# Two-layer hybrid decoder trunk: epsilon on VectorE, weight splits ahead of the last silu, last down products by column halves, GpSimd's residual products moved

## The chip, the cores and the metric

The kernel runs on one core of a Trainium2 chip, with its engines TensorE (PE), VectorE (DVE), ScalarE (ACT), GpSimd (POOL) and SyncE (SP, which only issues DMAs here). The metric is the device time of one execution in microseconds, the median of several runs.

## The reference

x is (1, 256, 1024) float32. Layer 0 mixes with a causal pooling, layer 1 with sliding-window attention. Each layer has three steps, so there are four feed-forward blocks (FFN 0 to 3, width 2816), two mixers and six layer norms (norm 0 to 5):

```python
def layer_norm(x, g, b):
    mu = jnp.mean(x, -1, keepdims=True); xc = x - mu
    var = jnp.mean(xc * xc, -1, keepdims=True)
    return xc * lax.rsqrt(var + LN_EPS) * g + b
def post_norm(x, sub, g, b):
    return layer_norm(DEEPNORM_ALPHA * x + sub, g, b)
for i in range(2):
    x = post_norm(x, 0.5 * swiglu(x, gate[i,0], up[i,0], down[i,0]), g[i,0], b[i,0])
    mix = pool_mixer(...) if i == 0 else swa_sink_attention(...)
    x = post_norm(x, mix, g[i,1], b[i,1])
    x = post_norm(x, 0.5 * swiglu(x, gate[i,1], up[i,1], down[i,1]), g[i,2], b[i,2])
```

## The kernel before, in words

The 256 tokens are two tiles, t = 0 and 1. To keep float32 accuracy nearly every product is made of three (`three`, L1057 to L1059): each operand is split into a high part (ACT copies it to fp32r: `g_hi` L459, `d_hi` L467, `xT_hi` L510, `hT_hi` L475) and a low part (DVE subtracts: `g_lo` L720, `d_lo` L724, `xT_lo` L806, `hT_lo` L733).

An FFN has 22 units of 128 columns. For each unit PE makes gate and up (48 products, `gate_up`), ACT takes the silu (L471), DVE multiplies it by the up half (`hf` L728), both split the result, and PE adds `ffn_down` into four PSUM banks: token tile t by column half h, 512 columns each, 3 products for each half. Units 0 and 1 use the raw weights with unsplit x (L1073) and need no split; units 2 to 21 do. On ACT and on DVE, `unit(f, u)` does, in program order: silu or `hf` of u, `g_split` of unit u+2, the split of h, `d_split` of unit u+1. After the last unit, `g_split(f+1, 2)` stands on ACT ahead of the transposed copies of the norm; on DVE its two halves stand as fillers in the norm (in norm 0 the two `d_split`s of the pooling weights do), between the variance and the wait for GpSimd.

SP issues every weight load in one fixed order (L263 on). Gate and up come as pairs of units (a chunk, 2 MB), down as pairs (1 MB). Each load waits for the split that frees its buffer. Between FFN 0 and FFN 1 the order is: pooling weights; gate/up of units 0 and 1 of FFN 1; down of units 0 and 1 (L252), which waits until `d_lo` of all 22 units of FFN 0 is done; then gate/up of units 2 and 3 (L245), which waits for `g_lo` of unit 21; then down of units 2 and 3.

A norm runs, for each t: DVE adds residual and product by column halves (L758) with `bn_stats` behind each (L759), then `bn_aggr` (L765); GpSimd adds epsilon (L356) and takes the power -1/2 (L358); DVE normalises both halves (L774), which count up `xn_done`; PE transposes (L1123) or, in the pool stage, multiplies by the band matrices (L890 for t=0, L894 for t=1); DVE and ACT copy the transposed tile with gain and bias (L800, L499). The pool stage then needs `xT_lo` from L843 on DVE. Norms 0 and 3 prepare the residual of the mixer on GpSimd: a product (`residual_mult`, L315) and a sum (`residual_add`, L319) for each t, of 1024 columns; `ax_done` counts them. At an FFN's end PE's order is: down of unit 21 for t=0, then of units 19, 20, 21 for t=1, each with both column halves.

Of the kernel before, what the change touches and what calls it, by code (L numbers as in the profile page):

```python
# [66 lines left out]
def trunk_kernel(nc, x, positions, ln_g, ln_b, w_gate, w_up, w_down, pool_w, pool_b, pool_scale,  # L67
# [8 lines left out]
    with ExitStack() as ctx:  # L76
# [70 lines left out]
        var_done = sem("var_done")  # L147
# [71 lines left out]
        prevT = xf[:, 1, 2:3, :]  # L219

# [80 lines left out]
        def _(gp):  # L301
# [19 lines left out]
            for n in range(6):  # L321
# [25 lines left out]
                if n == 3:  # L347

                    X, G, src = split_unit(None, 1)
                    gp.wait_ge(g_hi_done, 2 * X + 1)  # L350
                    gp.wait_ge(g_lo_done, 2 * X)
                    gp.tensor_tensor(g_half(g_lo, X, 0), src(G, 0), g_half(g_hi, X, 0).bitcast(f32), ALU.subtract).then_inc(g_lo_done, 1)
# [98 lines left out]
        def _(act):  # L451
# [25 lines left out]
            def unit(f, u, it=0):  # L477

                silu_of(f, u, it)
                if 1 <= u < UNITS - 2:  # L480
                    g_split(f, u + 2, it)
                elif f == 2 and u == UNITS - 2:
                    g_split(None, 0)
# [6 lines left out]
            def channel_major(e):  # L490

                for t in range(TT):
# [29 lines left out]
            for f in range(FFNS):  # L522
# [13 lines left out]
                if f == 0:  # L536
# [53 lines left out]
        def attention_dve(dve, link, note, g_split, d_split):  # L590
# [88 lines left out]
            g_split(None, 4)  # L679
            chunk(1, 0)  # L680
# [20 lines left out]
        def _(dve):  # L701
# [11 lines left out]
            def g_split(f, u, it=0, halves=(0, 1)):  # L713

                X, G, src = split_unit(f, u)
                for half in halves:
                    dve.wait_ge(g_hi_done, 2 * X + half + 1 + 8 * it)
                    if halves == (1,):
                        dve.wait_ge(g_lo_done, 2 * X + 1)
# [15 lines left out]
            def unit(f, u, it=0):  # L735

                h_of(f, u, it)
                if 1 <= u < UNITS - 2:
                    g_split(f, u + 2, it)
                elif f == 2 and u == UNITS - 2:  # L740
                    g_split(None, 0)
# [12 lines left out]
            def statistics(n, t, coef, early=None):  # L754

                for h in range(2):
                    dve.wait_ge(acc_done, 4 * n + 2 * t + h + 1)
                    link(dve.scalar_tensor_tensor(xn[:, t, HALVES[h]], ACC[t][h], coef, ax[:, t, HALVES[h]], ALU.mult, ALU.add))  # L758
                    last = dve.bn_stats(stats[:, h, :], xn[:, t, HALVES[h]])  # L759
                    if h == 0:  # L760
                        note(last)
                        if early:
                            early()
                link(last)
                dve.bn_aggr(mv[:, t, :], stats[:, :, :].rearrange("p a b -> p (a b)")).then_inc(stat_done, 1)  # L765

            def normalise(n, t, coef, filler=None, early=None):

                statistics(n, t, coef, early)
                if filler:  # L770
                    filler(t)
# [4 lines left out]

            def normalise_out(n, t, coef):

                statistics(n, t, coef)
# [41 lines left out]
            for f in range(FFNS):  # L821
# [14 lines left out]
                if f == 0:  # L836

                    for t in range(TT):
                        normalise(0, t, 0.5, filler=lambda t: d_split(D_POOL + t))
# [6 lines left out]
                    for t in range(TT):  # L846
                        dve.wait_ge(ax_done, 2 + t + 1)
                        normalise(1, t, 1.0, filler=lambda t: g_split(1, RAW_UNITS, halves=(t,)))
                        channel_major(1, t)
                    for t in range(TT):  # L850
                        x_lo(1, t)
                elif f == 1:
                    for t in range(TT):
                        normalise(2, t, 0.5, filler=lambda t: g_split(2, RAW_UNITS, halves=(t,)))
                        channel_major(2, t)
                    for t in range(TT):
                        x_lo(2, t)
                elif f == 2:

                    normalise(3, 0, 0.5, filler=lambda t: g_split(None, 1, halves=(1,)))  # L860
                    channel_major(QKV_EVENT, 0)
                    normalise(3, 1, 0.5, early=lambda: x_lo(QKV_EVENT, 0))
                    channel_major(QKV_EVENT, 1)
                    x_lo(QKV_EVENT, 1)
                    attention_dve(dve, link, note, g_split, d_split)
                    for t in range(TT):
                        dve.wait_ge(ax_done, 8 + t + 1)
                        normalise(4, t, 1.0, filler=lambda t: g_split(3, RAW_UNITS, halves=(t,)))
                        channel_major(4, t)
                    for t in range(TT):  # L870
                        x_lo(4, t)
# [40 lines left out]
        def attention_pe(pe, three, down, transposes, rest_of_ffn):  # L912
# [98 lines left out]
            rest_of_ffn()  # L1011
# [197 lines left out]
```

## Time and profile before

| | |
|---|---|
| median of 3 runs | 919.36 us (918.04 to 919.42) |
| span of the profiled execution (first to last instruction) | 916.1 us |
| median less that span (what lies around it; no time of its own is given for the profiled execution) | 3.26 us |
| PE busy | 875.6 us (96%) |
| DVE / ACT / POOL busy | 540.4 / 380.1 / 76.3 us |
| mean granted TensorE clock | 0.992 |

Busy times of PE are of pipelined instructions, so they overlap; the starts of neighbouring records tell the pace. In the timelines a row merges neighbouring instructions of one kind, and the bracket tells the idle time before it and who ended it.

### The profile page before, as it was taken

The numbers are of one execution on the slowest core, as the hardware profiler recorded it, in microseconds if no ns is written. First come the engines' busy times: TensorE is split into PE (matmuls) and PEld (weight loads), VectorE is DVE, ScalarE is ACT, GpSimd is POOL, SyncE is SP. The second block draws the span as 40 slices with busy tenths as digits, with TensorE's granted clock in tenths as the row PEclk, the third lists the DMA queues.
The fourth block names the chain that finished last, engine by engine and source line by source line (L and its number), as shares of the span: only waits on it lengthen the run. The fifth ranks groups of instructions, "written<-read, shape, count | busy, mean of one in ns | idle before, by whom it ended". The sixth has DMA issues, their size and how long they took to land.

```text
span 916.1 us, 14933 instructions
## 1 busy us (share of the span) xinstructions
PE 875.6 (96%) x5954; PEld 805.0 (88%) x5954; DVE 540.4 (59%) x758; ACT 380.1 (41%) x622; POOL 76.3 (8%) x71
## 2 busy tenths in 40 slices
PE   6999999997999999999999999988999999999995
PEld 6999999986999999998999999976766899999994
DVE  1764455488674455447665545568687775445445
ACT  2444344322444344333434433435575434434430
POOL 0020000066100000001040000023000100000001
PEclk9999999999999999999999999999999999999998
DMA  9886546254485555660865565450127096555501
GB/s 293 304 289 219 183 160 207 97 176 141 170 301 184 197 172 181 211 202 2 275 239 184 173 217 175 161 218 15 42 101 254 20 311 234 183 189 177 184 1 46
DMA packets 116275, 162.30 MB, mean 177 GB/s; under 512 B 3968, under 2 KB 97760, under 8 KB 116240
## 3 DMA queue, kind: packets, MB, share of 16 engines
q1 hardware_dynamic: 112656, 152.06, 49.2%
q0 software_dynamic: 2496, 9.44, 2.8%
q8 instruction: 24, 0.39, 0.2%
q10 hardware_dynamic: 1088, 0.32, 0.1%
q14 instruction: 11, 0.09, 0.0%
HBM read 160.75 MB, written 1.05 MB: 177 GB/s over the span
## 4 chain that ended last, share of the span: by engine, by line
PE 82%; DVE 10%; ACT 3%; POOL 2%; issue 1%; DMA 1%; SPq 0%; POOLq 0%; DVEq 0%; ACTq 0%
PE ps L1057 25%; PE ps L1058 25%; PE ps L1059 25%; PE ps L1073 5%; DVE stats L759 2%; DVE xn L758 2%; DMA raw_g<-in_ffn_w_up 1%; POOL rstd L356 1%; DVE xn L774 1%; PE ps L1123 1%; PE ps L943 1%; ACT silu L403 1%; PE ps L934 1%; PE ps L937 1%; POOL rstd L358 1%
## 5 line engine op out<-in xcount | busy, mean ns | idle before, releaser
L1059 PE MATMUL ps<-xT_hi,g_lo 128*128 128x256 f32 x1280 | 362.2, 283 | 0.0
L1058 PE MATMUL ps<-xT_lo,g_hi 128*128 128x256 f32 x1280 | 362.2, 283 | 0.0
L1057 PE MATMUL ps<-xT_hi,g_hi 128*128 128x256 f32 x1280 | 361.8, 283 | 0.0
L1057 PEld LDWEIGHTS ps<-xT_hi,g_hi 128*128 128x128 f32 x1280 | 245.4, 192 | 3.2
L1058 PEld LDWEIGHTS ps<-xT_lo,g_hi 128*128 128x128 f32 x1280 | 245.4, 192 | 3.1
L1059 PEld LDWEIGHTS ps<-xT_hi,g_lo 128*128 128x128 f32 x1280 | 245.4, 192 | 0.0
L720 DVE TENSOR_TENSOR g_lo<-raw_g,g_hi 128x1024 fp32r<-128x1024 f32 x171 | 206.5, 1247 | 42.0 <-ACT g_hi L459 41.9
L471 ACT ACTIVATE silu<-ps 128x256 f32<-128x256 f32 x88 | 33.8, 384 | 393.0 <-PE ps L1059 386.1
L728 DVE TENSOR_TENSOR hf<-silu,ps 128x256 f32<-128x256 f32 x88 | 37.0, 421 | 263.0 <-ACT silu L471 263.0
L459 ACT ACTIVATE g_hi<-raw_g 128x1024 fp32r<-128x1024 f32 x172 | 172.0, 1052 | 4.9 <-PE ps L943 4.4
L1057 PE MATMUL ps<-d_hi,hT_hi 128*128 128x512 f32 x352 | 138.7, 394 | 2.0 <-DVE hT_lo L733 2.0
L1058 PE MATMUL ps<-d_lo,hT_hi 128*128 128x512 f32 x352 | 137.9, 392 | 0.0
L1059 PE MATMUL ps<-d_hi,hT_lo 128*128 128x512 f32 x352 | 137.0, 389 | 0.0
L724 DVE TENSOR_TENSOR d_lo<-raw_d,d_hi 128x1024 fp32r<-128x1024 f32 x98 | 122.8, 1254 | 2.6 <-ACT d_hi L467 2.6
L467 ACT ACTIVATE d_hi<-raw_d 128x1024 fp32r<-128x1024 f32 x98 | 102.7, 1049 | 3.1 <-PE ps L1059 3.0
L1059 PEld LDWEIGHTS ps<-d_hi,hT_lo 128*128 128x128 f32 x352 | 66.1, 188 | 14.5
L1057 PEld LDWEIGHTS ps<-d_hi,hT_hi 128*128 128x128 f32 x352 | 66.4, 189 | 14.0 <-DVE hT_lo L733 2.4
L1058 PEld LDWEIGHTS ps<-d_lo,hT_hi 128*128 128x128 f32 x352 | 66.4, 189 | 10.6
L1073 PE MATMUL ps<-xf,raw_g 128*128 128x128 f32 x512 | 61.7, 282 | 3.8 <-DMA raw_g<-in_ffn_w_up 3.2
L1073 PEld LDWEIGHTS ps<-xf,raw_g 128*128 128x128 f32 x512 | 60.1, 197 | 5.4 <-DMA raw_g<-in_ffn_w_up 3.4
L733 DVE TENSOR_TENSOR hT_lo<-hf,hT_hi 128x256 fp32r<-128x256 f32 x88 | 43.5, 494 | 5.3 <-ACT hT_hi L475 5.3
L475 ACT ACTIVATE hT_hi<-hf 128x256 fp32r<-128x256 f32 x88 | 35.9, 408 | 11.9 <-DVE hf L728 11.9
(137 smaller groups left out, 548.9 us busy)
## 6 DMA issues: line engine op xcount, KB each, us to landing
raw_d<-in_ffn_w_down SPq DMA_DIRECT2D x87, 512.0 KB, 4.0
raw_g<-in_ffn_w_gate SPq DMA_DIRECT2D x43, 1024.0 KB, 5.3
raw_g<-in_ffn_w_up SPq DMA_DIRECT2D x43, 1024.0 KB, 7.8
raw_g<-in_attn_w_qkv SPq DMA_DIRECT2D x6, 1024.0 KB, 6.6
raw_d<-in_attn_w_o SPq DMA_DIRECT2D x8, 512.0 KB, 3.7
gb<-in_ln_g POOLq DMA_DIRECT2D x6, 512.0 KB, 5.2
gb<-in_ln_b POOLq DMA_DIRECT2D x6, 512.0 KB, 6.3
xn<-in_x SPq DMA_DIRECT2D x2, 512.0 KB, 7.2
```

What stands on the lines that cost most here:

```text
L459: act.activation(g_half(g_hi, X, half), src(G, half), ACT.Copy).then_inc(g_hi_done, 1)
L467: act.activation(d_hi[:, E % D_SLOTS, :], raw_d[:, (E // 2) % 2, E % 2, :], ACT.Copy).then_inc(d_hi_done, 1)
L471: act.activation(silu[:, u % 2, :], ps[:, WORK + u % 2, 0:S], ACT.Silu).then_inc(silu_done, 1)
L475: act.activation(hT_hi[:, (D0[f] + u) % D_SLOTS, :], hf[:, u % 2, :], ACT.Copy).then_inc(h_hi_done, 1)
L720: dve.tensor_tensor(g_half(g_lo, X, half), src(G, half), g_half(g_hi, X, half).bitcast(f32), ALU.subtract).then_inc(g_lo_done, 1)
L724: dve.tensor_tensor(d_lo[:, E % D_SLOTS, :], raw_d[:, (E // 2) % 2, E % 2, :], d_hi[:, E % D_SLOTS, :].bitcast(f32), ALU.subtract).then_in ...
L728: dve.tensor_tensor(hf[:, u % 2, :], silu[:, u % 2, :], ps[:, WORK + u % 2, S:2 * S], ALU.mult).then_inc(hf_done, 1)
L733: dve.tensor_tensor(hT_lo[:, slot, :], hf[:, u % 2, :], hT_hi[:, slot, :].bitcast(f32), ALU.subtract).then_inc(h_lo_done, 1)
L1057: pe.matmul(out_, l_hi, r_hi, start=start, stop=False)
L1058: pe.matmul(out_, l_hi, r_lo, start=False, stop=False)
L1059: return pe.matmul(out_, l_lo, r_hi, start=False, stop=stop)
L1073: last = pe.matmul(ps[:, WORK + u % 2, m * S + t * P:m * S + (t + 1) * P], raw_unit(G, m)[:, k, :], xf[:, t, k, :], start=i == 0, stop=i = ...
```

## The change

1. *Norm.* DVE adds epsilon (one instruction on 128x1 after `bn_aggr`), GpSimd only takes the power. `layer_norm` on DVE: the first residual sum of t=1 stands ahead of the wait for GpSimd of t=0; the fillers are gone from between the variance and that wait. The `d_split`s of the pooling weights follow norm 0, `g_split(3, 2)` follows norm 4 on DVE.
2. *Splits ahead of the last silu.* For FFN 0 and 1, ACT and DVE do `g_split(f+1, 2)` ahead of the silu and of `hf` of unit 21.
3. *Down products.* For t=1 the last three units go column half by column half. FFN 2's last product for t=1 is no longer held back behind the transposes; the first qkv products are reordered.
4. *GpSimd.* In norm 0 the sum of t=0, and product and sum of t=1, wait until t=1 is normalised. In norm 3, t=0's two are made ahead of t=1's power; t=1's two move to DVE in the attention part; the `g_lo` half that GpSimd made goes to DVE.
5. ACT splits x (`x_hi`) of t=0 straight behind its copies in norms 1, 2 and 4 too.

```diff
+        def next_split(f, u, it):
+            if 1 <= u < UNITS - 2:
+                return f, u + 2, it
+            if f == 2 and u == UNITS - 2:
+                return None, 0
+            if f < 2 and u == UNITS - 1:
+                return f + 1, RAW_UNITS
+            return None
...
@@ GpSimd
-                    gp.tensor_scalar(rstd[:, t, 0:1], mv[:, t, 1:2], EPS, None, ALU.add).then_inc(var_done, 1)
-                    gp.wait_ge(var_done, 2 * n + t + 1)
                     gp.tensor_tensor(rstd[:, t, 1:2], rstd[:, t, 0:1], mhalf[:, :], ALU.pow).then_inc(rstd_done, 1)
                     if step is not None and t == 0:
                         residual_mult(n, 0)
-                if step is not None:
+                        if n == 3:
+                            residual_add(step, 0)
+                if n == 0:
+                    gp.wait_ge(xn_done, 4)
                     residual_add(step, 0)
                     residual_mult(n, 1)
                     residual_add(step, 1)
@@ ScalarE, unit (VectorE's is changed likewise around h_of)
+                ahead = next_split(f, u, it)
+                if ahead and u == UNITS - 1:
+                    g_split(*ahead)
                 silu_of(f, u, it)
...
@@ VectorE
+            def layer_norm(n, coef, e=None, ready=None, behind_first=None, early_lo=False):
+                if ready:
+                    ready(0)
+                half_statistics(0, 0, residual_sum(n, 0, 0, coef))
+                variance(0, half_statistics(0, 1, residual_sum(n, 0, 1, coef)))
+                if ready:
+                    ready(1)
+                first = residual_sum(n, 1, 0, coef)
+                normalise(n, 0)
+                if e is not None:
+                    channel_major(e, 0)
+                if behind_first:
+                    behind_first()
+                half_statistics(1, 0, first)
+                variance(1, half_statistics(1, 1, residual_sum(n, 1, 1, coef)))
+                if early_lo:
+                    x_lo(e, 0)
+                normalise(n, 1)
...
-                        normalise(0, t, 0.5, filler=lambda t: d_split(D_POOL + t))
+                    layer_norm(0, 0.5)
+                    for j in range(POOL_UNITS):
+                        d_split(D_POOL + j)
...
@@ VectorE, attention, ahead of chunk(1, 0)
+            link(dve.tensor_tensor(ax[:, 1, :], xn[:, 1, :], gb[:, 0, :], ALU.mult))
+            dve.tensor_tensor(ax[:, 1, :], ax[:, 1, :], gb[:, 1, :], ALU.add).then_inc(ax_done, 1)
@@ TensorE
-                ffn_down(f, last_u + 1, (1,))
-                ffn_down(f, last_u + 2, (1,))
-                if f != 2:
-                    ffn_down(f, last_u + 3, (1,))
+                for h in range(2):
+                    for u in range(last_u + 1, UNITS):
+                        ffn_down(f, u, (1,), hs=(h,))
```

## Rows read from the trace of the kernel before

**Rows 1.** The page, chain that ended last, by engine (share of the span).

```profile
PE 82%; DVE 10%; ACT 3%; POOL 2%; issue 1%; DMA 1%; SPq 0%; POOLq 0%; DVEq 0%; ACTq 0%
```

**Rows 2.** Waits of PE: waiting line <- releaser: us in total, times, longest.

```profile
PE ps L1123 <- DVE xn L774: 7.5, 7, 2.1
...
PE ps L894 <- DVE xn L774: 4.0, 1, 4.0
```

**Rows 3.** Timeline of SP: start us, us, queue, line, issue.

```profile
199.17 0.82 SPq L252 DMA_DIRECT2D raw_d<-in_ffn_w_down  x2
...
200.50 0.58 SPq L245 DMA_DIRECT2D raw_g<-in_ffn_w_up  x1
...
400.62 0.58 SPq L245 DMA_DIRECT2D raw_g<-in_ffn_w_up  x1
```

**Rows 4.** Landing after issue: loads issued at 200.6 to 201, and at 400 to 401.

```profile
DMA to landing us min/median/max: 10.2/10.2/10.2
...
DMA to landing us min/median/max: 5.5/6.7/8.0
```

**Rows 5.** Timeline of ACT.

```profile
197.47 0.38 ACT L471 ACTIVATE silu<-ps 128x256 f32<-128x256 f32 x1 [1.15 <-PE ps L1059]
...
597.50 2.00 ACT L459 ACTIVATE g_hi<-raw_g 128x1024 fp32r<-128x1024 f32 x2
```

**Rows 6.** Timeline of DVE at three FFN tails.

```profile
197.93 1.21 DVE L724 TENSOR_TENSOR d_lo<-raw_d,d_hi 128x1024 fp32r<-128x1024 f32 x1
...
411.14 0.42 DVE L728 TENSOR_TENSOR hf<-silu,ps 128x256 f32<-128x256 f32 x1 [4.06 <-ACT silu L471]
412.04 0.42 DVE L733 TENSOR_TENSOR hT_lo<-hf,hT_hi 128x256 fp32r<-128x256 f32 x1 [0.48 <-ACT hT_hi L475]
...
598.59 2.36 DVE L720 TENSOR_TENSOR g_lo<-raw_g,g_hi 128x1024 fp32r<-128x1024 f32 x2 [0.53 <-ACT g_hi L459]
```

**Rows 7.** Timeline of PE: first record of unit 21's down product, f=0 and f=1.

```profile
200.96 0.39 PE L1057 MATMUL ps<-d_hi,hT_hi 128*128 128x512 f32 x1
...
413.27 0.39 PE L1057 MATMUL ps<-d_hi,hT_hi 128*128 128x512 f32 x1
```

**Rows 8.** Windows: stretch, us, busy of each engine, then PEclk.

```profile
210.00:222.00 12.00, 8.02 (x50) 7.47 (x50) 9.54 (x16) 4.92 (x10) 10.04 (x8) 0.86 0.25 89
```

**Rows 9.** Timeline of DVE, end of FFN 0 and the pool stage.

```profile
187.38 2.59 DVE L733 TENSOR_TENSOR hT_lo<-hf,hT_hi 128x256 fp32r<-128x256 f32 x1
...
204.61 0.21 DVE L765 BATCH_NORM_AGGREGATE mv<-stats 128x2 f32<-128x12 f32 x1
...
206.69 1.00 DVE L774 TENSOR_SCALAR xn<-xn,mv,rstd 128x512 f32<-128x512 f32 x2 [0.78 <-POOL rstd L358]
...
212.45 3.01 DVE L774 TENSOR_SCALAR xn<-xn,mv,rstd 128x512 f32<-128x512 f32 x2 [0.78 <-POOL rstd L358]
216.68 3.23 DVE L843 SCALAR_TENSOR_TENSOR xT_lo<-ps,lnT,xT_hi 128x256 fp32r<-128x256 f32 x8 [1.22 <-ACT xT_hi L544]
```

**Rows 10.** Timeline of POOL.

```profile
183.77 5.92 POOL L335 TENSOR_TENSOR raw_d<-raw_d,aux 128x1024 f32<-128x1024 f32 x2 [125.66 <-DMA raw_d<-in_pool_w]
...
204.97 1.02 POOL L356 TENSOR_SCALAR rstd<-mv 128x1 f32<-128x1 f32 x1 [7.25 <-DVE mv L765]
...
212.37 2.35 POOL L319 TENSOR_TENSOR ax<-ax,gb 128x1024 f32<-128x1024 f32 x1
...
619.48 0.23 POOL L356 TENSOR_SCALAR rstd<-mv 128x1 f32<-128x1 f32 x1 [3.38 <-DVE mv L765]
```

**Rows 11.** Timeline of PE at the norms after FFN 1 and after attention.

```profile
419.59 1.11 PE L1123 MATMUL ps<-cst,xn 128*128 128x128 f32 x8 [0.72 <-DVE xn L774]
...
426.99 1.12 PE L1123 MATMUL ps<-cst,xn 128*128 128x128 f32 x8 [0.34 <-DVE xn L774]
...
712.19 0.39 PE L1059 MATMUL ps<-d_hi,xT_lo 128*128 128x512 f32 x1
```

**Rows 12.** Timeline of DVE, second half of the norm before attention.

```profile
620.40 3.03 DVE L774 TENSOR_SCALAR xn<-xn,mv,rstd 128x512 f32<-128x512 f32 x2 [1.01 <-POOL rstd L358]
```

More of the change, by code:

```diff
@@ L477, in unit @@
             def unit(f, u, it=0):
+                ahead = next_split(f, u, it)
+                if ahead and u == UNITS - 1:
+                    g_split(*ahead)
                 silu_of(f, u, it)
[L480 to L483, printed above, removed]
+                if ahead and u < UNITS - 1:
+                    g_split(*ahead)
                 h_hi_of(f, u, it)
@@ L735, in unit @@
             def unit(f, u, it=0):
+                ahead = next_split(f, u, it)
+                if ahead and u == UNITS - 1:
+                    g_split(*ahead)
                 h_of(f, u, it)
[L738 to L741, printed above, removed]
+                if ahead and u < UNITS - 1:
+                    g_split(*ahead)
                 h_lo_of(f, u, it)
@@ L752, in _, with residual_sum, half_statistics, variance @@
             HALVES = [slice(512 * h, 512 * (h + 1)) for h in range(2)]
[L754 to L771, printed above, removed]
+            def residual_sum(n, t, h, coef):
+                dve.wait_ge(acc_done, 4 * n + 2 * t + h + 1)
+                return note(dve.scalar_tensor_tensor(xn[:, t, HALVES[h]], ACC[t][h], coef, ax[:, t, HALVES[h]], ALU.mult, ALU.add))
+            def half_statistics(t, h, summed):
+                dve.wait_ge(order, summed)
+                return note(dve.bn_stats(stats[:, h, :], xn[:, t, HALVES[h]]))
+            def variance(t, counted):
+                dve.wait_ge(order, counted)
+                link(dve.bn_aggr(mv[:, t, :], stats[:, :, :].rearrange("p a b -> p (a b)")))
+                dve.tensor_scalar(rstd[:, t, 0:1], mv[:, t, 1:2], EPS, None, ALU.add).then_inc(stat_done, 1)
+            def normalise(n, t):
                 dve.wait_ge(rstd_done, 2 * n + t + 1)
@@ L845, in _ @@
                         last.then_inc(u_lo_done, 1)
[L846 to L851, printed above, removed]
-                elif f == 1:
[L853 to L857, printed above, removed]
-                elif f == 2:
[L860 to L864, printed above, removed]
-                    attention_dve(dve, link, note, g_split, d_split)
[L866 to L871, printed above, removed]
+                    layer_norm(1, 1.0, 1, ready=lambda t: dve.wait_ge(ax_done, 2 + t + 1))
+                elif f == 1:
+                    layer_norm(2, 0.5, 2)
+                elif f == 2:
+                    g_split(None, 1, halves=(0,))
+                    layer_norm(3, 0.5, QKV_EVENT, behind_first=lambda: g_split(None, 1, halves=(1,)), early_lo=True)
+                    attention_dve(dve, link, note, g_split, d_split)
+                    layer_norm(4, 1.0, 4, ready=lambda t: dve.wait_ge(ax_done, 8 + t + 1))
+                    g_split(3, RAW_UNITS)
                 else:
@@ L1097, in down @@
                 for t in ts:
-                    for h in range(2):
+                    for h in hs:
                         w_hi, w_lo = (b[:, E % D_SLOTS, 512 * h:512 * (h + 1)] for b in (d_hi, d_lo))
```

50 lines of the change are left out of this document (25 added, 25 removed).

## The prediction

> **What bounds the kernel now.** I read the page's chain first. TensorE has 82% of it [rows 1], so between the norms nothing but product time counts. In the tails the chain leaves TensorE, and there a stall is worth its full length. PE's waits name them: 7.5 us for the normalised x ahead of the transposes in seven waits, and 4.0 us ahead of the second half of the pool product [rows 2]. Some 12 us is therefore what shorter norms could give at most. Then I read SP's timeline and the landings, since two weight splits are moved ahead of an instruction that TensorE's last products need, and last the tails on DVE, GpSimd and PE. All steps below are in times of the profiled execution (span 916.1 us); the median of the runs is 3.26 us more, and that is added at the end unchanged.
>
> **Step 1, the split ahead of the last silu, FFN 0: +14.5 us.** The moved `g_split(1, 2)` needs the raw weights of units 2 and 3 of FFN 1. SP has one order. The down load ahead of them waits for `d_lo` of unit 21. That subtraction runs from 197.93 for 1.21 us, to 199.14 [rows 6], and SP issues at 199.17; the up half of the chunk needed follows at 200.50 [rows 3] and lands 10.2 us later, at 210.7 [rows 4]. Nothing of the change makes `d_lo` of unit 21 earlier: it stands in unit 20, and what slows it (GpSimd, below) stays. The silu of unit 21, though, runs at 197.47 today [rows 5]. In the new order it stands behind a wait for 210.7 on an engine that works in order; so does `hf` on DVE. Behind the silu wait `hf`, the h splits, and unit 21's down product, which starts at 200.96 today [rows 7]. New:
> - 210.7 landing, + 2.0 for the two `g_hi` (597.50 to 599.50 [rows 5]) = 212.7;
> - DVE's two `g_lo` end 1.45 us behind those (600.95 against 599.50 [rows 5, 6]) = 214.15;
> - `hf` to the end of `hT_lo` takes 1.32 us (411.14 to 412.46 [rows 6]) = 215.5.
>
> PE starts at 215.5 instead of 200.96: 14.5 us. The products of units 18 to 20 are in both orders done before that, and the 18 products of t=1 stand behind unit 21 for t=0 in PE's order, so nothing hides it. Bounds: 13 us if the load lands 1.5 us sooner (the landings of 10.2 and 8.0 us [rows 4] differ by what is loaded beside them, here 1 MB of down weights), 16 us if later.
>
> **Step 2, TensorE's clock after that idle: +0.9 us.** After the stall in the pool stage the stretch 210 to 222 had a mean granted clock of 0.86 [rows 8]: of 12 us, 12 x 0.14 x 2 = 3.4 us at 1.2 instead of 2.4 GHz. An idle of 14.5 us should cost the same. 24 products take 5.6 us (413.27 to 418.87, which is 0.72 before 419.59 [rows 7, 11]), so they end at 215.5 + 5.6 + 1.7 = 222.8. DVE would want the last of them for its fourth sum at 222.1 (aggregate's end 204.82 + 14.5, + 1.0 for the power, + 1.0 for normalising, + 0.7 and the links [rows 9]). With the hand-over that is 0.9 us. Bounds 0 and 2.5. The Trainium skill (TensorE: Matmul & The Clock Gate, Part 1) calls the half clock the default state, from which activity releases the engine. By that the first product already runs at 1.2 GHz; in this trace the fall was seen only behind a 4 us idle, and no row shows 14 us ahead of work.
>
> **Step 3, norm 0: the gain is 3 us on DVE, and GpSimd takes most of it back.** GpSimd's epsilon instruction takes 1.02 us at 204.97 while DVE's filler runs, and 0.23 at 619.48 without one [rows 10]. Without filler and epsilon on GpSimd, aggregate to normalise takes 1.0 instead of 1.87 us (204.82 to 206.69 [rows 9]): I price DVE's epsilon like the GpSimd one it replaces, at 0.2 to 0.3, nearest the 0.21 of the aggregate [rows 9]. The second normalise took 3.01 instead of 1.00 us [rows 9], since GpSimd's sum of 2.35 ran beside it [rows 10]; that sum is moved behind it. New: fourth sum 222.95, statistics and aggregate to 224.65, power to 225.65, normalised at 226.65 (before: 215.46).
> Now both engines start at once. DVE has two `d_lo` (1.2 each [rows 6]), both inputs in SBUF; GpSimd has sum, product, sum (2.35 each [rows 10]). The rows say that such a pair excludes each other: `hT_lo`, 0.42 us alone, took 2.59 beside GpSimd's product [rows 6, 9, 10]. Alternating, DVE gets 1.2, GpSimd 2.35, DVE 1.2 = 4.75 us instead of 2.4. Then `xT_lo` from PSUM (L843): 231.4 to 234.65, before 216.68 to 219.91 [rows 9]. (GpSimd's second sum ends 9.5 us behind 226.65, at 236.15; DVE asks for it at about 238, so that added wait is covered, with 1.9 us to spare.) The pool stage ends **14.75 us late**, steps 1 to 3 together: step 3 alone is -0.65.
> The Trainium skill (SBUF — State Buffer, Who interferes with whom) says that a VectorE instruction with two SBUF inputs and a GpSimd instruction that reads SBUF lock each other out for a whole instruction, whichever issues first. That order speaks against the change here; by it the sum is the 4.75 used, and 7.1 if GpSimd got two turns running.
>
> **Step 4, norm 1: -1.2.** Its first half is 0.87 sooner by the same term. In the second half PE waited 0.34 (the like of 426.99 [rows 11]; here 0.4). The first sum ahead of the wait and the dropped filler bring that normalise over 2 us forward, but PE has 48 raw records in between, so only the 0.34 counts. Running: +13.55.
>
> **Step 5, FFN 1's end and norm 2: -1.0.** The same move costs little here: the load is issued at 400.62 [rows 3] and lands 8.0 later [rows 4], at 408.6. `g_hi` to 410.65, `g_lo` to 412.1, `hT_lo` to 413.45; PE wants it at 413.27 [rows 7], so +0.2. Against it -0.87 and -0.34 [rows 11]. PE's products end at 418.87 and the transposes can now follow at once, so the first term is about fully paid. By halves, the t=1 column half 0 is ready when DVE has done t=0; without that the early sum would hold DVE.
>
> **Step 6, norm 3 and attention: -0.4 (-2 to +1).** The second normalise took 3.03 us beside GpSimd [rows 12]; that 2 us goes, and qkv starts some 2 us sooner. But DVE gets product and sum of t=1, 1.2 us each like a `d_lo` [rows 6], in front of chunk (1, 0), where it is already the late engine. What is left is about 0.4.
>
> **Step 7, norm 4: -0.5.** Here the last product of t=1 is at 712.19 [rows 11] and not split by halves; the early sum waits for its column half 0 (about 711.8) and delays the normalise of t=0 to nearly its old time. 0.15, and the 0.34 behind. DVE's `g_split(3, 2)`, now behind the norm, delays `hT_lo` of unit 0 by 2.4 us, inside PE's 9 us of raw products. **Norm 5: 0.** Its scalings on DVE lie over the power already.
>
> **Sum.** 13.55 - 1.0 - 0.4 - 0.5 = +11.65; span 927.75, with 3.26 around it **931.0 us**.
>
> **Rivals.**
> A, other side: *the split finds its data*. If what the new split waits for has landed before unit 21's silu, as it nearly has in FFN 1, steps 1 and 2 vanish, and FFN 0's end costs nothing. Then norm 0 ends 0.9 sooner, pool and norm 1 add 1.55: -2.45, and -1.15 for norm 2 without its 0.2, -0.4, -0.5: 914.9 us. It decides at a landing before about 205 (TensorE reaches the product at 200.96, and the gains pay for 4 us). Against it: SP's order, and a chunk issued only at 200.50. For it: only that I might misread which load the split needs. 0.08.
> B: *the collision of step 3 does not come* or the clock does not fall. DVE keeps its 2.4 us: -2.35, or -0.9: 928.6 or 930.1. The rows speak against it. 0.1.
> C: *further waits*: GpSimd's chain takes two turns running, attention's DVE work is paid in full, the clock stays low longer: 934 to 936. 0.07.
> D: *more is given back*: DVE's leaner norms and the refilled queue give 3 to 6 us more than I count, 925 to 928. 0.07.
> The forecast itself has 0.68, own range 928.6 to 933.5.
>
> Range 926.5 to 934.5: it leaves out A and the tails of C and D. This kernel's runs spread by 0.15%, so 0.2% (1.8 us) is what can be told from no change. Faster 0.08 (A), same 0.02 (a landing near 205), slower 0.90.
>
> **What would show it.** Step 1: ACT's silu of unit 21 of FFN 0 behind two `g_hi` at about 213, released by the DMA of up weights, and PE idle for 14 to 15 us with the granted clock at half behind it. Step 2: products at half pace at 215.5. Step 3: the two pool `d_lo` take near 4.7 us together, beside GpSimd's sum; L843 near 231. Steps 4 and 5: L1123 of t=1 follows the raw products without a gap. Step 6: two more DVE instructions of 1.2 us ahead of chunk (1, 0). It is wrong if the silu of unit 21 runs near 197: then the time is below 919.

## The result, and the profile after

The changed kernel takes 933.69 us (median of 4 runs, 932.2 to 934.95), the kernel before beside it 919.39 (4 runs, 918.04 to 920.16): so the medians lie 14.3 us apart. The measured ratio is a little less than that of the two medians: 1.0146 with a 95% interval of 1.013 to 1.0163, which is 13.4 us (12.0 to 15.0). The forecast was 931.0, and 933.7 lies in its range. The profiled execution has a span of 933.1 us and is the longest of the four; its start (first instruction to the first down product) took 31.3 us where the one of before took 28.2. That start varies between 28.2 and 31.4 us over all traces here, with code that none of the kernels touches. I therefore compare traces by stretches between marks and leave the start out.

First the chain that ended last, by engine, as the page of the changed kernel has it (before: [rows 1]).

```profile
PE 84%; DVE 7%; ACT 3%; DMA 2%; POOL 1%; issue 1%; SPq 1%; DVEq 0%; ACTq 0%
```

VectorE's share fell from 10% to 7%, DMA's went from 1% to 2%. Next the waits of PE (waiting line, releaser: us in total, times, longest), which answer to [rows 2]:

```profile
PE ps L1078 <- DVE hT_lo L739: 16.6, 3, 14.6
PE ps L1094 <- DMA raw_g<-in_ffn_w_up: 4.9, 2, 4.1
...
PE ps L953 <- ACT xT_hi L515: 4.2, 2, 2.1
PE ps L1144 <- DVE xn L781: 3.6, 2, 2.9
...
PE ps L953 <- DVE g_lo L726: 1.6, 1, 1.6
PE ps L1078 <- DVE xT_lo L878: 1.5, 1, 1.5
```

The 7.5 us in seven waits for the normalised x have become 3.6 in two, and the pool product's 4.0 us are gone. One new wait of 14.6 us outweighs both. Its cause is read upwards through three engines. SP's timeline (start, us, queue, line, issue), answering to [rows 3]:

```profile
202.26 0.82 SPq L261 DMA_DIRECT2D raw_d<-in_ffn_w_down  x2
...
203.59 0.58 SPq L254 DMA_DIRECT2D raw_g<-in_ffn_w_up  x1
```

ACT's timeline at the end of FFN 0 and, last row, in the attention stage (start, us, engine, line, operation; in brackets the idle time before and who ended it), answering to [rows 5]:

```profile
214.06 2.00 ACT L463 ACTIVATE g_hi<-raw_g 128x1024 fp32r<-128x1024 f32 x2 [14.66 <-DMA raw_g<-in_ffn_w_up]
215.97 0.36 ACT L475 ACTIVATE silu<-ps 128x256 f32<-128x256 f32 x1
...
648.63 2.00 ACT L463 ACTIVATE g_hi<-raw_g 128x1024 fp32r<-128x1024 f32 x2 [6.06 <-PE ps L962]
```

The load issued at 203.59 lands at 214.06, and only then come the two `g_hi` and, behind them in ACT's order, the silu that had its input long before. The silu ran at 197.47 before. DVE's timeline, answering to [rows 6, 9]:

```profile
215.15 2.36 DVE L726 TENSOR_TENSOR g_lo<-raw_g,g_hi 128x1024 fp32r<-128x1024 f32 x2 [12.93 <-ACT g_hi L463]
...
218.33 0.42 DVE L739 TENSOR_TENSOR hT_lo<-hf,hT_hi 128x256 fp32r<-128x256 f32 x1 [0.48 <-ACT hT_hi L479]
...
223.50 0.15 DVE L775 TENSOR_SCALAR rstd<-mv 128x1 f32<-128x1 f32 x1
...
229.40 1.00 DVE L781 TENSOR_SCALAR xn<-xn,mv,rstd 128x512 f32<-128x512 f32 x2 [0.67 <-POOL rstd L359]
230.31 2.35 DVE L730 TENSOR_TENSOR d_lo<-raw_d,d_hi 128x1024 fp32r<-128x1024 f32 x2
232.59 3.22 DVE L878 SCALAR_TENSOR_TENSOR xT_lo<-ps,lnT,xT_hi 128x256 fp32r<-128x256 f32 x8
...
239.78 0.69 DVE L764 SCALAR_TENSOR_TENSOR xn<-ps,ax 128x512 f32<-128x512 f32 x1 [0.90 <-POOL ax L328]
241.84 1.00 DVE L781 TENSOR_SCALAR xn<-xn,mv,rstd 128x512 f32<-128x512 f32 x2 [1.36 <-POOL rstd L359]
```

The normalise that took 3.01 us takes 1.00, and the two `d_lo` behind it take 2.35 together. GpSimd's sum waited for both of them (POOL's timeline, answering to [rows 10]):

```profile
230.48 4.42 POOL L328 TENSOR_TENSOR ax<-ax,gb 128x1024 f32<-128x1024 f32 x1 [1.12 <-DVE xn L781]
234.87 2.40 POOL L324 TENSOR_TENSOR ax<-xn,gb 128x1024 f32<-128x1024 f32 x1
237.35 2.40 POOL L328 TENSOR_TENSOR ax<-ax,gb 128x1024 f32<-128x1024 f32 x1
240.04 0.64 POOL L336 DMA_DIRECT2D gb<-in_ln_g  x1 [0.30 <-POOL ax L328]
240.68 0.54 POOL L337 DMA_DIRECT2D gb<-in_ln_b  x1
241.24 0.56 POOL L359 TENSOR_TENSOR rstd<-rstd,mhalf 128x1 f32<-128x1 f32 x1
```

Its chain ends at 239.75, and DVE's sum of t=1 at 239.78 waits 0.90 for it. Then come two DMA issues, 1.18 us, ahead of the power that norm 1's first half has wanted since 238.9 (epsilon at 238.73). PE waits for the normalised x that comes of it (PE's timeline, answering to [rows 7, 11]):

```profile
218.81 0.79 PE L1078 MATMUL ps<-d_hi,hT_hi 128*128 128x512 f32 x1 [14.60 <-DVE hT_lo L739]
219.40 0.63 PE L1079 MATMUL ps<-d_lo,hT_hi 128*128 128x512 f32 x1
...
223.66 0.39 PE L1080 MATMUL ps<-d_hi,hT_lo 128*128 128x512 f32 x1
...
242.64 1.06 PE L1144 MATMUL ps<-cst,xn 128*128 128x128 f32 x8 [2.93 <-DVE xn L781]
243.87 7.34 PE L1094 MATMUL ps<-xf,raw_g 128*128 128x128 f32 x48 [0.16 <-DVE xf L834]
...
651.00 0.50 PE L953 MATMUL ps<-g_hi,xT_hi 128*128 128x512 f32 x1 [1.56 <-DVE g_lo L726]
```

A product's record is 0.63 us long up to 223.2 and 0.39 from 223.66 on. The windows of this kernel (stretch, us, busy of PE, PEld, DVE, ACT, POOL with instructions, then PEclk, DMA share, GB/s) answer to [rows 8]. They show the half clock behind the long stall, in norm 1 and, twice, in the attention part:

```profile
219.00:220.00 1.00, 1.00 (x3) 0.81 (x4) 0.00 (x0) 0.24 (x1) 0.00 (x0) 0.50 0.00 0
...
224.00:225.00 1.00, 1.00 (x6) 0.82 (x5) 0.22 (x1) 0.00 (x0) 0.37 (x1) 1.00 0.00 0
...
245.00:246.00 1.00, 1.00 (x7) 1.00 (x6) 0.97 (x3) 1.00 (x3) 0.00 (x0) 0.50 0.07 29
...
633.00:637.00 4.00, 4.00 (x12) 3.13 (x11) 3.77 (x9) 0.00 (x0) 2.57 (x2) 0.57 0.85 263
...
643.00:647.00 4.00, 4.00 (x12) 3.12 (x11) 2.17 (x10) 0.00 (x0) 0.00 (x0) 0.57 0.01 4
```

The whole in one table, from DVE's and PE's timelines of each profile. A mark "sum k" is the start of norm k's first residual sum, "raw end" the start of the last of PE's raw products of the next FFN, "qkv" the first qkv product, "scores" the first DVE instruction on the scores. All in us; e1 is the first experiment below, e12 the last.

| stretch | before | after | difference | e1 | e12 |
|---|---|---|---|---|---|
| first down product to sum 0 | 173.62 | 189.17 | +15.55 | 173.58 | 173.58 |
| sum 0 to sum 1 (norm 0, pool) | 18.46 | 15.23 | -3.23 | 14.26 | 14.26 |
| sum 1 to raw end (norm 1) | 22.82 | 25.02 | +2.20 | 24.79 | 22.05 |
| raw end to sum 2 | 171.04 | 171.11 | +0.07 | 171.35 | 171.38 |
| sum 2 to raw end (norm 2) | 22.62 | 21.09 | -1.53 | 21.12 | 21.10 |
| raw end to sum 3 | 171.02 | 171.04 | +0.02 | 171.03 | 171.02 |
| sum 3 to qkv (norm 3) | 8.68 | 7.74 | -0.94 | 7.76 | 9.16 |
| qkv to scores | 33.63 | 37.42 | +3.79 | 38.92 | 33.80 |
| scores to sum 4 | 57.82 | 56.73 | -1.09 | 56.77 | 56.79 |
| sum 4 to raw end (norm 4) | 22.62 | 21.88 | -0.74 | 21.88 | 21.88 |
| raw end to the end | 185.53 | 185.38 | -0.15 | 185.39 | 185.37 |

The differences add up to +13.95; the medians differ by 14.3.

### The profile page after: what moved, and what is told of

Its sections match the earlier page's. It is cut to its first block, busy times and chain, and to the rows that moved or that the text cites. A ratio compares the mean times of both kernels' runs of the same rounds, so it can differ in the third digit from the quotient of the medians.

```text
span 933.1 us, 14931 instructions
## 1 busy us (share of the span) xinstructions
PE 880.7 (94%) x5954; PEld 810.0 (87%) x5954; DVE 539.1 (58%) x773; ACT 380.0 (41%) x622; POOL 60.5 (6%) x56
## 4 chain that ended last, share of the span: by engine, by line
PE 84%; DVE 7%; ACT 3%; DMA 2%; POOL 1%; issue 1%; SPq 1%; DVEq 0%; ACTq 0%
PE ps L1078 25%; PE ps L1079 25%; PE ps L1080 24%; PE ps L1094 6%; DMA raw_g<-in_ffn_w_up 2%; PE ps L953 1%; PE ps L956 1%; PE ps L1144 1%; POOL ax L328 1%; PE ps L962 1%; ACT hf L407 1%; DVE g_lo L726 1%; DVE d_lo L730 1%; DVE hT_lo L739 1%; DVE sm L640 1%
## 5 line engine op out<-in xcount | busy, mean ns | idle before, releaser
L1078 PE MATMUL ps<-d_hi,hT_hi 128*128 128x512 f32 x352 | 139.8, 397 | 16.6 <-DVE hT_lo L739 16.6
L1094 PE MATMUL ps<-xf,raw_g 128*128 128x128 f32 x512 | 64.3, 289 | 5.4 <-DMA raw_g<-in_ffn_w_up 4.9
L1094 PEld LDWEIGHTS ps<-xf,raw_g 128*128 128x128 f32 x512 | 62.5, 204 | 7.2 <-DMA raw_g<-in_ffn_w_up 5.2
L479 ACT ACTIVATE hT_hi<-hf 128x256 fp32r<-128x256 f32 x88 | 35.9, 408 | 13.4 <-DVE hf L734 13.4
```

The lines of the kernel that those rows point to most:

```text
L479: act.activation(hT_hi[:, (D0[f] + u) % D_SLOTS, :], hf[:, u % 2, :], ACT.Copy).then_inc(h_hi_done, 1)
L1078: pe.matmul(out_, l_hi, r_hi, start=start, stop=False)
L1094: last = pe.matmul(ps[:, WORK + u % 2, m * S + t * P:m * S + (t + 1) * P], raw_unit(G, m)[:, k, :], xf[:, t, k, :], start=i == 0, stop=i = ...
```

## Experiments

Nine of the experiments start from e1, so that the 15 us don't lie over what they test. Ratios are to the kernel before, measured beside each, with a 95% interval of 0.0012 to 0.0022 to each side (1.1 to 2.0 us). The stretches tell finer things than the times, but each is of one execution, and falls of the clock lie over them. The diffs are shortened, and some lines joined. No experiment tests by itself the first residual sum of t=1 ahead of the wait, or point 5 of the change.

**e1: the early split of FFN 0 alone put back.**

```diff
-            if f < 2 and u == UNITS - 1:
+            if f == 1 and u == UNITS - 1:
                 return f + 1, RAW_UNITS
```
(on ACT the split stands, as in the kernel before, ahead of the copies of norm 1's transposes; on DVE it stands behind norm 1, where the kernel before had its halves inside the norm)

> The changed kernel, with the split of FFN 1's units 2 and 3 put back behind the pool stage on ScalarE and behind norm 1 on VectorE; FFN 1's own early split stays. Theory (the silu of FFN 0's unit 21 waits for a load that lands 14 us later): TensorE's idle of 14.6 us ahead of unit 21's down product goes, and with it the half clock behind it: 933.7 - 14.7 - 1.2 = 917.8 us, between 916 and 920. Rival (the early split costs 5 us at most, the rest is lost in norm 1 and in the attention part, where the changed trace has 2.0 and some 2.5 us of new waits): 927 or more. Rival 2 (the rest of the change brings what I first summed, 4.5 us): 915.

Measured: 918.24 us, ratio 0.9965 [0.9953, 0.9978]. ACT's timeline:

```profile
199.14 0.38 ACT L475 ACTIVATE silu<-ps 128x256 f32<-128x256 f32 x1 [1.17 <-PE ps L1082]
```

The silu waits for its product alone, the first stretch is back at 173.58, the half clock behind it is gone. The split's place is the whole slowdown. What the rest of the change gains together is less sure: 3.2 us by the ratio (2.0 to 4.3), 1.9 us by the two medians (918.24 against 920.12 beside it), 1.0 us by the stretches, in which e1 has 10 us of half clock in the attention part.

**e2: the early split kept, its load issued earlier.** SP's order for FFN 1 is changed alone:

```diff
+                if f == 1:
+                    load_gate_up(1, 0); load_gate_up(1, 1)
+                    load_down(1, 0); load_down(1, 1)
```
(the loop behind it then starts at the third chunk)

> The changed kernel with the early split kept, but SyncE issues gate/up of FFN 1's units 2 and 3 ahead of the down weights of its units 0 and 1. Theory (only the arrival of the load costs): it is issued some 12 us sooner, at about 190.5 of the changed trace, lands near 200, the silu follows at about 202, TensorE idles about 1 us: 1 us above the kernel with the late split, 917 to 920. Rival (the two splits in front of the silu cost by standing there, whatever has landed): 2 x 1.05 us on ScalarE and 2.4 us on VectorE, 922 to 924. Rival 2 (the down weights now arrive late and stall FFN 1): above 925.

Measured: 918.84, ratio 0.9982 [0.9969, 0.9995]. SP's timeline, then ACT's:

```profile
189.46 0.58 SPq L254 DMA_DIRECT2D raw_g<-in_ffn_w_up  x1
```

```profile
197.75 1.99 ACT L468 ACTIVATE g_hi<-raw_g 128x1024 fp32r<-128x1024 f32 x2
199.65 0.36 ACT L480 ACTIVATE silu<-ps 128x256 f32<-128x256 f32 x1
```

The split stands in the same place and costs 1.9 us (173.58 to 175.48) instead of 15.6. So it is the load's time of issue, behind the down load, and not the split's own work; and rival A, "the split finds its data", describes this kernel.

**e3: the early splits alone, in the kernel before.**

```diff
+                if f < 2 and u == UNITS - 1:
+                    g_split(f + 1, RAW_UNITS)
                 silu_of(f, u, it)
```
(the same on DVE; the fillers of norms 1 and 2, which were these splits, are gone)

> The kernel before, with nothing changed but the early splits for FFN 1 and FFN 2 (their filler places in norms 1 and 2 are then empty). Theory: +14.7 us of idle and +1 to 2 us of half clock, less about 2 x 1.2 us because GpSimd's epsilon no longer waits for a filler in norms 1 and 2: 919.4 + 13.5 to 14.5 = 933 to 934. Rival (the early split costs 5 us at most, the rest of the change costs the remainder): 922 to 925.

Measured: 932.05, ratio 1.0117 [1.0101, 1.0134]. ACT's timeline:

```profile
212.01 2.00 ACT L459 ACTIVATE g_hi<-raw_g 128x1024 fp32r<-128x1024 f32 x2 [14.30 <-DMA raw_g<-in_ffn_w_up]
```

The same wait; first stretch 188.84, norm 0 and pool 19.67. Of the three kernels with the early split (changed, e2, e3) the two whose load is late are slow, whatever the norms do.

**e4: e1, with GpSimd's two DMA issues behind the power of t=0 in norm 1.**

```diff
-                load_gb()          # for every n, ahead of the power
+                if n != 1: load_gb()
                 ...ALU.pow).then_inc(rstd_done, 1)
+                    if n == 1 and t == 0: load_gb()
```

> The kernel with the late split (ratio 0.9965 to the kernel before, some 3.2 us faster), with one more edit: GpSimd issues the two loads of norm 1's gain and bias behind the power of t=0, not ahead of it. Theory (norm 1 lost 2.9 us of TensorE idle because GpSimd's queue was full: two sums and a product end at 221.7, then 1.2 us of DMA issue, then the power): the normalise of t=0 comes 1.3 us sooner; if the shorter idle also keeps TensorE's clock up, another 1.5 us. So 1.3 to 2.8 us faster than the late split, ratio 0.9935 to 0.995. Rival (TensorE has work in between, as in norm 2, and hides it): no change, 0.9965.

Measured: 915.67, ratio 0.994 [0.9919, 0.9962]. POOL's timeline:

```profile
222.15 0.55 POOL L362 TENSOR_TENSOR rstd<-rstd,mhalf 128x1 f32<-128x1 f32 x1
222.65 0.75 POOL L337 DMA_DIRECT2D gb<-in_ln_g  x1
```

Sum 1 to raw end falls from 24.79 to 23.62, by the two issues' 1.2 us. They were on the path. What is left above the 22.82 of before is half clock, 3.4 us of it here.

**e5: e1, with the qkv products of t=1 half by half, as before.** **e6: e1, with FFN 2's nine last products of column half 1 held behind the transposes of t=0**, as the kernel before held a product back.

```diff
-            qkv(0, 0, 1, part=0); qkv(0, 1, 1, part=0)
-            qkv(0, 0, 1, part=1).then_inc(g_used, 1); qkv(0, 1, 1, part=1)
+            qkv(0, 0, 1).then_inc(g_used, 1); qkv(0, 1, 1)
```

```diff
             transposes(e, 0)
+            for u in range(last_u + 1, UNITS): ffn_down(2, u, (1,), hs=(1,))
             qkv(0, 0, 0, part=0, d_counted=True)
```

> The late split, and the first qkv products of t=1 again half by half, all 12 products of the first half of the weights ahead of the second half's. Theory (by taking both halves' products with the high part first, the changed order frees the first half of the weights 2.7 us later, ScalarE's split behind it starts at 630.6 instead of 628, and TensorE waits 1.6 us for g_lo): 1.5 to 2.5 us faster than the late split, ratio 0.994 to 0.995. Rival (VectorE is the late engine of that stretch with its two added instructions, and its queue decides): 0 to 0.5 us.

> The late split, and FFN 2's last nine down products for t=1 (column half 1) held back behind the transposes of norm 3's t=0. Theory (TensorE idles 2.1 us behind those transposes, and its clock is at half for 3.3 us from 614.0, which costs 1.6 us; the held products fill the idle time, as products of that kind did before the change): the clock stays up, qkv of t=0 ends 1.6 us sooner, of which the attention part keeps 1 to 1.6: ratio 0.995. Rival (the idle time only moves to ahead of the transposes and the clock falls anyway): 0.9965, same as the late split.

Measured: e5 915.98, ratio 0.9954 [0.9938, 0.9971]; e6 914.98, 0.9948 [0.9928, 0.9968]. qkv to scores falls from 38.92 to 35.51 in e5, and PE's wait for `g_lo` is gone from its list: ACT's `g_hi` at 648.63 above had waited for the high parts of both halves. Of that fall some 1.9 us are order (the changed kernel, e2, e4, e8, e9 and e10, with e1's attention code and as much half clock as e5, have 37.4), the rest is 3.4 us less at half clock. In e6 it falls to 34.28, with the clock at full level through the stretch (windows, then PE's timeline):

```profile
613.00:635.00 22.00, 18.28 (x81) 13.90 (x80) 16.61 (x37) 10.87 (x20) 4.87 (x3) 1.00 0.28 96
```

```profile
610.80 1.11 PE L1147 MATMUL ps<-cst,xn 128*128 128x128 f32 x8 [1.84 <-DVE xn L782]
```

The nine products fill the first of the two waits of 2.11 us for `xT_hi`, but a wait of 1.84 us appears ahead of the transposes instead, which e1 does not have: the idle time only moved, as the first half of the rival said. What e6's trace gains is the clock, and e7's trace (next), with nothing held back, has the same stretch at 34.25, also without a fall. So it is not shown that holding the products keeps the clock up, or that norm 3's 0.9 us caused the falls; the ratios of e5 and e6 don't settle it either, since their intervals overlap that of e1. The mean clock of e6's six runs was 0.987 to 0.993 and of e1's 0.987 to 0.989, but e4, with e1's attention code, had 0.988 to 0.993.

**e7: e1, with GpSimd's order of before in norm 0.**

```diff
-                    gp.wait_ge(xn_done, 4)
                     residual_add(step, 0)
```

> The late split, and GpSimd's sum of t=0 in norm 0 again straight behind the power of t=1, without waiting until t=1 is normalised. Theory (the move only shifts the collision: 2.0 us lost in the second normalise against 0.9 us for the early sum in norm 1 plus GpSimd's late power there): the normalise of t=1 takes 3.0 instead of 1.0 us, norm 1 gets about 2 us back and the clock may stay up: within 1 us of the late split, ratio 0.9955 to 0.9975. Rival (the move is worth its full 2 us): 0.9985.

Measured: 920.39, ratio 0.9995 [0.9978, 1.0013]. DVE's timeline, then POOL's:

```profile
211.50 3.01 DVE L781 TENSOR_SCALAR xn<-xn,mv,rstd 128x512 f32<-128x512 f32 x2 [0.67 <-POOL rstd L359]
214.44 4.50 DVE L730 TENSOR_TENSOR d_lo<-raw_d,d_hi 128x1024 fp32r<-128x1024 f32 x2
```

```profile
211.44 2.34 POOL L328 TENSOR_TENSOR ax<-ax,gb 128x1024 f32<-128x1024 f32 x1
...
214.59 3.26 POOL L324 TENSOR_TENSOR ax<-xn,gb 128x1024 f32<-128x1024 f32 x1 [0.82 <-DVE xn L781]
```

Both collisions are back: 2.0 us on the normalise, 2.15 on the two `d_lo`. Sum 0 to sum 1 is 19.26, 5.0 us more than in e1 (where the clock did not fall, as it did here); sum 1 to raw end is 2.4 less, since GpSimd is done in time. The moved sum is worth 2.6 us net in these traces, and 2.8 by the ratios (0.9995 against 0.9965). My theory, that the move only shifts the collision, was wrong.

**e8: e1, with epsilon on GpSimd again. e9: e1, with the `g_lo` halves back as fillers ahead of the wait in norms 1 and 4. e10: e1, with the last down products by units.**

```diff
+                    gp.tensor_scalar(rstd[:, t, 0:1], mv[:, t, 1:2], EPS, None, ALU.add)   # e8
```
```diff
+                if filler: filler(t)     # e9: g_split(1, 2, halves=(t,)), g_split(3, 2, halves=(t,))
```
```diff
-                for h in range(2):       # e10
                     for u in range(last_u + 1, UNITS):
-                        ffn_down(f, u, (1,), hs=(h,))
+                        ffn_down(f, u, (1,))
```

> The late split, and epsilon again on GpSimd, ahead of its power; the fillers stay out of the way. Theory (GpSimd's epsilon took 1.08 us only because VectorE's filler ran beside it; alone it takes 0.23): the instruction costs on either engine about the same (0.23 + 0.08 against 0.15 + 0.15 us), so 0 to 0.5 us from the late split, ratio 0.9960 to 0.9975. Rival (epsilon on VectorE is itself worth the 0.87 us for each half norm): 5 us slower than the late split, ratio above 1.001.

> The late split, and in norms 1 and 4 a half of the next g_lo split stands again between the variance and the wait for GpSimd's power, with epsilon on VectorE. Theory (the filler holds GpSimd's power back until it ends, about 0.9 us for each half; of it only the first halves reach TensorE): 1 to 2 us slower than the late split, ratio 0.9975 to 0.999. Rival (a filler in the gap is hidden, the gain came from epsilon): no change, 0.9965.

> The late split, and the last down products of t=1 again unit by unit, both column halves of each, in all four FFNs. Theory (the early residual sum of t=1 then waits for column half 0 until 0.7 us before TensorE's end, some 1.4 us later, and holds the normalise of t=0, which stands behind it, by about 0.9 us): norms 0, 2 and 3 lose 0.5 to 0.9 us each, 1.5 to 2.5 us slower, ratio 0.998 to 0.9995. Rival (VectorE has slack there): 0.9965.

Measured: e8 919.39, ratio 0.9996 [0.9983, 1.0009]; e9 917.46, 0.9969 [0.9957, 0.9982]; e10 920.11, 0.9999 [0.9985, 1.0013]. In e8 the norms' stretches are longer by 0.45, 0.06, 0.15 and 0.14, 0.8 us in all; the other 1.6 of its trace is norm 1, 26.40 instead of 24.79, where the half clock lasted 6.9 us instead of 3.5. So 0.8 us is shown for the epsilon. By the ratio e8 is 2.9 us slower than e1, which misses the 0.9960 to 0.9975 that I expected without reaching the rival's 1.001; the other 2 us I take for clock, and whether this edit brings falls on is not shown. e10 shows +0.77, +0.80 and +0.76 us in norms 0, 2 and 3: the column halves bring 0.8 us a norm, because DVE's early sum of t=1 finds its half (in e10's norm 0 it waits 0.91 us for PE, in e1's not at all). Their sum is 2.3 us, within the 1.5 to 2.5 that I expected; the ratio says 3.1. e9 is a miss of mine: I expected 1 to 2 us and the trace has +0.10 in norm 1 and +0.15 in norm 4. DVE's timeline of e9:

```profile
223.31 1.22 DVE L727 TENSOR_TENSOR g_lo<-raw_g,g_hi 128x1024 fp32r<-128x1024 f32 x1 [0.90 <-POOL ax L328]
...
225.37 1.00 DVE L782 TENSOR_SCALAR xn<-xn,mv,rstd 128x512 f32<-128x512 f32 x2 [0.23 <-POOL rstd L359]
```

In norm 1 the filler fits into the wait for GpSimd's late power; dropping the fillers in these two norms is worth 0.1 and 0.15 us.

**e11: e1, with norm 3's residual of t=1 back on GpSimd.**

```diff
-            dve: tensor_tensor(ax[:, 1], xn[:, 1], gb[:, 0], mult); tensor_tensor(ax[:, 1], ax[:, 1], gb[:, 1], add)
+            gp:  residual_mult(n, 1); residual_add(step, 1)
```

> The late split, and norm 3's residual product and sum of t=1 on GpSimd again, now behind the normalise of t=1 (they were on VectorE in the attention part, 2.4 us ahead of chunk (1, 0)). Theory (VectorE is the late engine there, TensorE waits 1.2 us for chunk (1, 0), and the two x_lo splits of t=1 collide less than before since they stand 6 us behind): 1 to 2.4 us faster, ratio 0.994 to 0.9955. Rival (the products on GpSimd hold up VectorE's splits of x again, 2 us, as in the kernel before): 0.9965 or above.

Measured: 918.35, ratio 0.9973 [0.9961, 0.9986], no gain over e1; I had expected one. qkv to scores is 38.29 against 38.92, at the same 10 us of half clock, so DVE's two instructions cost that stretch 0.6 us, not the 2.5 of their length. But scores to sum 4 goes from 56.77 to 57.80, the value of before. That is a fall of the clock (windows of e11, then of the kernel before):

```profile
703.40:706.70 3.30, 3.30 (x8) 2.28 (x7) 2.40 (x3) 0.00 (x0) 0.00 (x0) 0.50 0.38 119
```

```profile
700.80:704.30 3.50, 3.50 (x10) 2.44 (x9) 2.73 (x4) 0.15 (x1) 0.00 (x0) 0.51 0.46 146
```

Up to the wait of 1.88 us for DVE's `hf` ahead of the fall, e11 is 0.3 us ahead of e1. The three traces with this residual on GpSimd (before, e3, e11) have the fall and some 57.8, the eleven others have neither. Why it comes with the residual stays open.

**e12: e1 with e4, e5 and e6 together.**

> The change with three parts altered together: the split of FFN 1's first gate and up back in its old place (as in e1_late_split), GpSimd's issues of the next gamma and beta behind norm 1's first pow (e4_gb_late), the qkv products of the second half half by half (e5_t1_order), and FFN 2's nine last products of column half 1 behind the transposes of the three-way products (e6_held). Theory: the three gains lie in different places and add up. Their stretches by the traces: norm 1 -1.2 us, the attention's qkv stretch -1.9 (order) and -3.1 (held) against e1_late_split's, so first sum of norm 1 to the raw products' end about 23.6, and qkv to the first scores 32.5 to 34; total 5 to 6.2 us below e1_late_split, 910.5 to 913.5 on this scale where the kernel before has 919.4: ratio 0.9895 to 0.9925. Rival 1 (the order and the held products cover the same wait): the qkv stretch stays at 34.3 to 35.5 and the ratio is 0.993 to 0.995. Rival 2 (the removed wait returns as a half clock elsewhere, as between n1 and the raw products of e6_held, 26.1 instead of 24.8): 0.992 to 0.995 with that stretch above 25.

Measured: 912.36 us (6 runs, 909.71 to 913.34), the kernel before beside it 919.19 (11 runs), ratio 0.9916 [0.9898, 0.9935]. This beats both kernels, by 6.8 us (7.7 by the ratio) and by some 21 us. Norm 1's stretch is 22.05: 1.2 us from the issues, and 1.5 because no half clock came. The attention's two stretches together are 42.96, against 46.68 in e1, 43.26 in e5, 42.03 in e6. Order and held products don't add up here, because the clock fell where e6's did not (PE's timeline, then windows). At the same 6.8 us of half clock, e12 has only 0.3 us on e5, which holds nothing back:

```profile
608.08 1.91 PE L1150 MATMUL ps<-cst,xn 128*128 128x128 f32 x8 [1.84 <-DVE xn L787]
```

```profile
608.00:610.00 2.00, 1.93 (x9) 1.93 (x10) 1.31 (x5) 0.00 (x0) 1.44 (x1) 0.55 0.00 0
```

Rival 2 of its expectation holds in kind, in another place than it named; the ratio still came out as the theory's.

## Why the prediction was right, point by point

**Step 1 (+14.5), right.** +15.55 in the first stretch, +15.6 against e1. The inputs held too: SP issued at 203.59 in a trace whose start is 3.1 us later, which is the forecast's 200.50, and the landing took 10.45 us instead of 10.2. The 2.0 for the `g_hi` are exact (ACT's row at 214.06). The silu runs between `g_hi` and `hf`, but DVE's `g_lo` cover it; PE's wait of 14.60 stands where 14.5 was forecast. The rest of the 15.55, 0.8, is slow product pace: from PE's start to DVE's first sum 1.68 us (218.81 to 220.49) instead of 0.87 (200.96 [rows 7] to 201.83).

**Step 2 (+0.9), right in kind, mis-sized: 1.8.** The half clock lies over the products from 218.81 to some 223.6, 4.8 us, less than the 5.6 + 1.7 I let it run over and more than the 3.4 of [rows 8]. 0.8 us of its cost lie in the first stretch, as just said, and 0.97 in the next: 15.23 against 14.26 in e1, whose clock did not fall there. By the Trainium skill (TensorE: Matmul & The Clock Gate, Part 1), cited in the prediction, the first product behind the idle already runs at half clock; the trace agrees, with 0.79 and then 0.63 us. The prediction's remark that the trace of before had a fall only behind a 4 us idle was a misreading: it has another at 700.8, behind waits of at most 1.9 us (the window under e11). From that row I could have known that short waits can be followed by half clock, which steps 4 and 6 put at nothing.

**Step 3 (-0.65), wrong in size; the term that failed is "4.75 instead of 2.4".** The two `d_lo` took 2.35 us: both went ahead of GpSimd's sum, which took 4.42. By itself step 3 is -4.2 (18.46 to 14.26 in e1): the -0.65, those 2.35, and 1.2 more, of which the column halves are 0.77 (e10); I had seen their use for norm 2 and not counted it here. The last 0.4 are open; the trace of before had half clock at 216.2 to 219.6 in this stretch, e1 had none. That DVE keeps its 2.4 us was rival B's first half. The Trainium skill (SBUF — State Buffer, Who interferes with whom) calls the shared port pair an exclusive lock and says that issue order decides who blocks. That is not contradicted: DVE's row starts at 230.31, GpSimd's at 230.48. What I added to it, that the two take turns, did not hold there; in e7 they did take turns.

**Step 4 (-1.2), wrong: +2.2.** The statement that failed is "that added wait is covered, with 1.9 us to spare". GpSimd's chain was as long as forecast (9.35 us behind the normalise, 229.40 + 1.00 to 239.75, against 9.5). What was wrong was when DVE asks: I had it at 238, with DVE held up by the collision; taken back by the 3.1 us of the start, DVE asked at 235.8 (238.88 in the trace), 2.2 us sooner. With GpSimd's end 0.5 us later than forecast, the 1.9 to spare became a wait of 0.9. And I had not counted the two DMA issues in GpSimd's queue ahead of the power, 1.18 us (e4 shows 1.17). Behind the wait of 2.93 the clock fell: 48 raw products in 7.34 us, where e12's trace has 5.79 at full clock. The three, 0.9 + 1.2 + 1.5 = 3.6, are about the 3.4 between forecast and measurement. Without such a fall and without the issues the stretch is 22.05 in e12, 0.8 us under before.

**Step 5 (-1.0), about right:** -1.46 (+0.07 and -1.53). The early split in FFN 1 costs 0.07 in this trace and 0.2 to 0.35 in those of e1, e3 and e12; I had 0.2.

**Step 6 (-0.4, bounds -2 to +1), wrong: +1.76.** The normalise gave 0.94 ahead of qkv, not 2. I took DVE's queue for the late engine and priced its two instructions; e11 shows 0.6 for them. The term that failed is the clock, which I had put at nothing: the two falls, 6.8 us at half, cost 3.1 of the 3.79, since the same stretch is 37.4 us in e8 and 34.25 in e7, whose attention code is the same and in which the clock did not fall. At full clock all edits together cost it 0.6 (34.25 against 33.63), so norm 3 up to the scores would be 0.3 us shorter than before. The product order costs 1.9 us where the falls come (e5 against the 37.4); what it costs at full clock no trace isolates. The -1.09 behind the scores is the fall at 700.8 of before, which this trace lacks.

**Step 7 (-0.5) and norm 5 (0), right:** -0.74 and -0.15.

**The sum.** Forecast +11.65, traces +13.95. The 3.26 us added for what lies around the span was no such thing: each execution with a recorded time and span took 1.7 to 1.9 us more than its span, and the other 1.4 say that the profiled execution of before was a short one, with a start of 28.2 us. For the changed kernel the median is only 0.6 above the profiled span, whose start is 3.1 us longer; the two nearly cancel, which is luck. Against the forecast, steps 1 and 2 are 1.1 us dearer, step 3 3.55 cheaper, step 4 3.4 dearer, step 5 0.45 cheaper, step 6 2.15 dearer, step 7 and norm 5 0.4 cheaper: together 2.3. The likeliest case held for its large term; the small steps erred by more than their own sizes, and that they mostly cancelled is luck. The early split behind its late load costs 16.6 us in the first two stretches (against e1) and 15.0 over the whole trace, in which e1 has one more fall in the attention part; all else gains between 1.0 us (stretches) and 3.2 us (ratio).

## What to carry to other kernels

Before moving work that reads a load ahead of something that does not, find in which place of the DMA queue's order that load is issued, and from which instruction's end it can be: the in-order engine pays the whole distance, as here with 15 us for 2 us of work, while with the loads reordered the same place cost 1.9 us. When a collision of two engines is taken off one of them, look at the other's chain to its next consumer, DMA issues included. Short waits around transposes can cost more than their length through the clock, and whether they do changes from one execution to the next: compare such an edit over several executions, or at an equal amount of half clock.

## What the runs showed of the hardware

- *Who gets the turn.* GpSimd's sum, issued 0.17 us behind the first of two `d_lo`, waited for both (4.42 us, and 4.43 in e4 and e8). In e7 GpSimd's product, issued 0.15 us behind the first, ran between the two (DVE 4.50, GpSimd 3.26). What decides stays open.
- *The clock falls on kernels alike in different places.* Behind the same 2.11 us wait ahead of qkv, half clock adds up to 6.8 us in most traces, 10 in e1 and e11, none in e7. It makes a difference of 1.5 us in norm 1 and of 3 us in attention that no edit explains, so a single trace cannot price such an edit. The Trainium skill (TensorE: Matmul & The Clock Gate, Part 1) says that one kernel shows different counts of slow products from run to run. No kernel was profiled twice here, but the mean clock of each execution agrees: e2's twelve runs go from 916.19 us at 0.993 to 921.25 us at 0.985.
- *A tiny instruction on GpSimd waits for some of DVE's work and not for other.* Epsilon on 128x1 took 1.02 us beside DVE's `d_lo`, which reads two operands in SBUF [rows 10]. It took 0.23 in e8's norm 0, while DVE ran a residual sum that reads one of its two from PSUM (POOL's timeline, then DVE's):

```profile
204.95 0.23 POOL L360 TENSOR_SCALAR rstd<-mv 128x1 f32<-128x1 f32 x1 [7.22 <-DVE mv L778]
```

```profile
204.70 0.64 DVE L768 SCALAR_TENSOR_TENSOR xn<-ps,ax 128x512 f32<-128x512 f32 x1
```
